# Second block's expert pairs in another order, and their loads written out

## The reference

```python
h2 = rms_norm_2(x, norm2_g)
# group: argmax of h2 @ w_group + b_group; in it the top 2 of h2 @ w_expert + b_expert
g, u = h2 @ w_gate[group, e], h2 @ w_up[group, e]      # 1024 -> 256
x = x + sum(gate[e] * ((silu(g) * u) @ w_down[group, e]))   # 256 -> 1024
```

## Time and profile before

| | |
|---|---|
| median of 3 runs | 1562.14 us |
| lowest and highest | 1559.04 and 1563.06 us |
| time of the profiled execution | 1566.48 us |
| its span in the trace | 1564.7 us |
| PE busy | 1338.8 us, 86% |
| DVE, ACT, POOL busy | 454.9, 379.1, 47.8 us |
| moved from memory | 476.71 MB, 306 GB/s over the span |

### The profile page before, as it was taken

The page is one execution under the profiler, slowest core; times in us unless marked ns, Lnnn a source line. Parts: engine busy times, 40 slices in busy tenths (PEclk is TensorE's granted clock), DMA queues, the critical chain, the costliest instruction groups (busy, mean ns, idle before and its releaser), DMA issues.

```text
span 1564.7 us, 31839 instructions
## 1 busy us (share of the span) xinstructions
PE 1338.8 (86%) x12460; PEld 697.1 (45%) x12461; DVE 454.9 (29%) x1358; ACT 379.1 (24%) x730; POOL 47.8 (3%) x74
## 2 busy tenths in 40 slices
PE   4999987988666786799999898987899899999986
PEld 3655444454232343355556544433337454443432
DVE  1102466442121121233344533111122544212112
ACT  2101235112111111122223322222132432222212
POOL 1100030000000000000000000000000000000000
PEclk8899999999898899899999899999899999999988
DMA  9968412769999999989784277999992435679996
GB/s 360 359 253 265 113 28 95 272 254 418 417 419 416 419 417 418 418 359 417 299 314 161 81 282 279 418 417 418 418 396 94 166 129 217 255 289 419 416 419 254
DMA packets 104049, 479.45 MB, mean 306 GB/s; under 512 B 9521, under 2 KB 20110, under 8 KB 70910
## 3 DMA queue, kind: packets, MB, share of 16 engines
q1 hardware_dynamic: 100256, 469.66, 76.0%
q0 software_dynamic: 2688, 7.43, 1.7%
q10 hardware_dynamic: 1054, 1.63, 0.3%
HBM read 476.71 MB, written 1.98 MB: 306 GB/s over the span
## 4 chain that ended last, share of the span: by engine, by line
PE 58%; SPq 18%; DMA 12%; DVE 6%; issue 4%; ACT 2%; ACTq 0%; DVEq 0%; PEldq 0%
SPq L518 18%; PE psum L1199 6%; PE psum L1938 6%; DMA store<-in_w_up 6%; PE psum L774 5%; PE psum L1190 5%; PE psum L1175 5%; PE psum L1148 4%; DMA store<-in_w_expert_up 4%; PE psum L1210 3%; PE psum L1934 3%; PE psum L1217 2%; PE psum L1470 2%; PE psum L1458 2%; PE psum L1503 1%
## 5 line engine op out<-in xcount | busy, mean ns | idle before, releaser
L1190 PE MATMUL psum<-store 128*32 128x256 f32 x2624 | 176.7, 411 | 58.9 <-DMA store<-in_w_expert_up 57.5
L1199 PE MATMUL psum<-store 128*32 128x256 f32 x2432 | 156.4, 414 | 25.0 <-DMA store<-in_w_up 23.1
L1348 DVE TENSOR_TENSOR store<-store,psum 128x128 f32<-128x128 f32 x79 | 22.7, 288 | 464.8 <-ACT store L1280 464.4
L1190 PEld LDWEIGHTS psum<-store 128*32 128x32 f32 x2624 | 79.8, 115 | 139.4 <-DMA store<-in_w_expert_up 85.7
L1175 PE MATMUL psum<-store 32*128 32x256 f32 (+1 forms) x992 | 129.5, 478 | 2.0 <-ACT store L1286 1.4
L1148 PE MATMUL psum<-xn,store 128*32 128x256 f32 (+1 forms) x992 | 130.0, 490 | 1.3 <-DVE store L1311 1.2
L1199 PEld LDWEIGHTS psum<-store 128*32 128x32 f32 x2432 | 88.7, 119 | 83.1 <-issue 34.5
L1280 ACT ACTIVATE store<-psum 128x128 f32<-128x128 f32 x79 | 21.9, 277 | 405.2 <-PE psum L1190 276.8
L1280 ACT ACT_TABLE_LOAD x79 | 101.4, 1283 | 52.7 <-issue 52.0
L1938 PE MATMUL psum<-store 128*128 128x512 f32 x224 | 97.7, 593 | 0.0
L1175 PEld LDWEIGHTS psum<-store 32*128 32x128 f32 (+1 forms) x992 | 59.2, 191 | 75.2 <-issue 69.6
(11 more groups left out here) (357 smaller groups left out, 1441.4 us busy)
## 6 DMA issues: line engine op xcount, KB each, us to landing
store<-in_w_expert_up SPq DMA_DIRECT2D x128, 1024.0 KB, 22.3
store<-in_w_expert_down SPq DMA_DIRECT2D x64, 1024.0 KB, 22.4
store<-in_w_gate SPq DMA_DIRECT2D x64, 1024.0 KB, 17.8
store<-in_w_up SPq DMA_DIRECT2D x64, 1024.0 KB, 19.6
store<-in_w_down SPq DMA_DIRECT2D x64, 1024.0 KB, 20.2
store<-in_w_mod SPq DMA_DIRECT2D x12, 2048.0 KB, 14.3
store<-in_w_in SPq DMA_DIRECT2D x6, 2048.0 KB, 12.2
store<-in_w_out SPq DMA_DIRECT2D x6, 2048.0 KB, 15.2
```

What stands on the lines that cost most here:

```text
L1190: mm = pe.matmul(out_(j), chosen_rows(k, 0), wt[:, kk, :, j, :], start=(k == 0), stop=(k == KD - 1))
L1199: mm = pe.matmul(out_(j), chosen_rows(k, e), wt, start=(k == 0), stop=(k == KD - 1))
```

## The change

In both layers of the second block the rounds take the pairs in the order 0, 4, 8, 12, 1, 5, 9, 13, 2, 6, 10, 14, 3, 7, 11, 15: one pair of each group in turn. The loads read their sources by that order; `ranks`, the gates and `extra` are written in that order too, by views that permute the columns. Two vector operations (L1024 and L1043) become two each, one for each tile of 128 tokens, for the second block alone. The ranks' first step writes into `chosen` in place. For the second block the loop over loads on SP is replaced by 72 loads in a row, with addresses known beforehand; the waits before them count the same.

```diff
-        def expert_loads(sp, plan, sources, turned, dense_done, adds):
+        def expert_loads(sp, plan, sources, turned, dense_done, adds, order=None):
             stage = plan.stage(sources[0].shape[0])
+            nth = order or list(range(stage.rounds))
...
-                load(i, j, sources[j][r])
+                load(i, j, sources[j][nth[r]])
...
-                load(2, j, sources[j][3])
-            turns = (stage.rounds - 1) // TURN - 1
-            with sp.Fori(0, turns) as turn:
+                load(2, j, sources[j][nth[3]])
+            turns = 0 if order else (stage.rounds - 1) // TURN - 1
+            if turns:
+                with sp.Fori(0, turns) as turn:
...
             for r in range(TURN * (turns + 1) + 1, stage.rounds):
                 for j, src in enumerate(sources):
                     sp.wait_ge(*stage.freed(r - TURN, j))
-                    load((r - 1) % TURN, j, src[r])
+                    load((r - 1) % TURN, j, src[nth[r]])
...
-            link(dve.scalar_tensor_tensor(ranks[:, 0:NT, 0:NE], r[:, 0:NT, :], 1.0, chosen, ALU.add, ALU.mult))
-            link(dve.tensor_scalar(ranks[:, 0:NT, 0:NE], ranks[:, 0:NT, 0:NE], -1.0, None, ALU.add))
+            link(dve.scalar_tensor_tensor(chosen, r[:, 0:NT, :], 1.0, chosen, ALU.add, ALU.mult))
+            if which == 1:
+                link(dve.tensor_scalar(ranks[:, 0:NT, 0:NE], chosen, -1.0, None, ALU.add))
+            else:
+                for t in range(NT):
+                    ins_ = dve.tensor_scalar(woven(ranks[:, t, 0:NE]), chosen[:, t, :].rearrange("p (g b e) -> p g b e", g=NG, b=NG),
+                                             -1.0, None, ALU.add)
+                link(ins_)
+
+        def woven(x):
+
+            return x.rearrange("p (b g e) -> p g b e", b=NG, g=NG)
...
+            else:
+                for t in range(NT):
+                    ins_ = dve.tensor_tensor(woven(ranks[:, NT + t, 0:NE]), rest4[:, t].rearrange("p g (b e) -> p g b e", e=2),
+                                             first5[:, t, 0, 0:NG].unsqueeze(2).unsqueeze(3).broadcast_to([P, NG, NG, 2]), ALU.mult)
+                link(ins_)
...
-                link(dve.tensor_reduce(extra_m[:, 0:NE // at_once], extra_f.rearrange("p (b e) -> p b e", e=at_once), AX,
-                                       ALU.max))
+                link(dve.tensor_reduce(extra_m.rearrange("p (b g) -> p g b", b=NG),
+                                       extra_f.rearrange("p (g b e) -> p g b e", g=NG, b=NG), AX, ALU.max))
...
-                expert_loads(sp, plan, second_sources(layer), (sems["q_sb"], NT * (1 + layer)), 2 + layer, NT * (3 + 2 * layer))
+                pairs = [NG * g + b for b in range(NG) for g in range(NG)]
+                expert_loads(sp, plan, second_sources(layer), (sems["q_sb"], NT * (1 + layer)), 2 + layer, NT * (3 + 2 * layer),
+                             pairs)
```

More of the change, by code:

```diff
@@ L543, in expert_loads @@
                 sp.wait_ge(*stage.freed(0, j))
-                load(2, j, sources[j][3])
-            turns = (stage.rounds - 1) // TURN - 1
-            with sp.Fori(0, turns) as turn:
[L547 to L552, removed]
+                load(2, j, sources[j][nth[3]])
+            turns = 0 if order else (stage.rounds - 1) // TURN - 1
+            if turns:
+                with sp.Fori(0, turns) as turn:
+                    for i in range(TURN):
+                        for j, src in enumerate(sources):
+                            sem, count = stage.freed(1 + i, j)
+                            sp.wait_ge(sem, turn * (TURN * stage.used(j)[1]) + count)
+                            load(i, j, src[bass.ds(turn * TURN + (TURN + 1 + i), 1)][0])
             for r in range(TURN * (turns + 1) + 1, stage.rounds):
@@ L1022, in route_dve, with route_gates_dve @@
             r = ps[5][:, 0:3 * NE].rearrange("p (n e) -> p n e", e=NE)
-            link(dve.scalar_tensor_tensor(ranks[:, 0:NT, 0:NE], r[:, 0:NT, :], 1.0, chosen, ALU.add, ALU.mult))
-            link(dve.tensor_scalar(ranks[:, 0:NT, 0:NE], ranks[:, 0:NT, 0:NE], -1.0, None, ALU.add))
+            link(dve.scalar_tensor_tensor(chosen, r[:, 0:NT, :], 1.0, chosen, ALU.add, ALU.mult))
[8 more added lines that the diff above has]
+            return x.rearrange("p (b g e) -> p g b e", b=NG, g=NG)
         def group_marks():
             return first5[:, :, 0, 0:NG].unsqueeze(3).broadcast_to([P, NT, NG, EG])
-        def route_gates_dve(dve, at, link):
+        def route_gates_dve(dve, at, link, which):
             wide = lambda x: x.unsqueeze(2).unsqueeze(3).broadcast_to([P, NT, NG, EG])
@@ L1042, in route_gates_dve @@
             link(dve.tensor_tensor(rest4, rest4, second4, ALU.add))
-            link(dve.tensor_tensor(ranks[:, NT:, 0:NE].rearrange("p t (g e) -> p t g e", g=NG), rest4, group_marks(),
-                                   ALU.mult))
+            if which == 1:
+                link(dve.tensor_tensor(ranks[:, NT:, 0:NE].rearrange("p t (g e) -> p t g e", g=NG), rest4, group_marks(),
+                                       ALU.mult))
+            else:
[3 more added lines that the diff above has]
+                link(ins_)
         def extra_rounds_dve(dve, at, link, which):
@@ L1370, in experts_dve @@
                 dve.wait_ge(sems["gate_moe_in"], 64)
-            route_gates_dve(dve, at, link)
+            route_gates_dve(dve, at, link, which)
             current(dve.tensor_copy(it[:, NT:, :], ranks[:, NT:, 0:at_once]))
```

## The result

The changed kernel takes 1538.78 us (median of 4 runs, 1538.19 to 1540.42); the one before took 1562.60 us beside it (1559.04 to 1563.62). The ratio is 0.9843, with a 95% interval of 0.9821 to 0.9864. Timed again in two later sessions it gave 0.9868 (0.9848 to 0.9888) and 0.9847 (0.9830 to 0.9864). A median of 1540.2 had been forecast, within a range of 1534 to 1549.

The account below looks back on a forecast made before the run. Transfers and the matmul engine were taken to bound the kernel in turn. Layer 1's 15.9 us plus layer 0's 6.6 less 0.6 for vector operations gave 21.9 us, so a median of 1540.2 us, range 1534 to 1549.

Parts of the forecast that it names:

- What bounds: Second block's rounds: PE and transfers bound in turn; six double rounds (pairs needing a second pass), two in layer 0, four in layer 1.
- Part one: Layer 1's rounds: spreading double rounds starts loads sooner, PE runs through, and the last pass starts 15.9 us earlier.
- The tightest place: Layer 1, behind double round 4: round 7's loads go out at 1385.4, 0.5 us before the stream needs them.
- Part two: Layer 0's rounds: double rounds at 11 and 15 let round 15 start 8.3 us earlier, less 1.7: 6.6 us.
- slow first pass: Layer 0's round 15: a pass that waited for data has slower up matmuls, taking back 1.7 us.
- cushion of 4.6 us: Layer 0: lag from double round 11 that can grow by 4.6 us before it touches round 15.
- Part three: Loads on SP, 72 a layer: removing their loop and register offset is priced at nothing, under 2 us if cover fails.
- Part four: Vector engine, ranks and gate product in two operations each: 0.15 us at two places in two layers, 0.6 us cost.
- The sum: Whole kernel: 15.9+6.6-0.6 = 21.9 us gain, profiled span to 1542.8, median to 1540.2.
- slower transfers: Rival, weight loads of both layers: new address order slows the stream, 1554 at 392 GB/s, 1600 at 350; chance 0.05.
- a layer 0 without gain: Rival, layer 0's rounds: only layer 1 pays, layer 0 gives 0 to 3 us, time 1544 to 1547; chance 0.07.
- signs of being wrong: Full-stretch rate below 416 to 419 GB/s, layer 1 waiting on w_up after round 7, or 155.1 us between layers changing over 1 us.

Follow-up runs that it names:

- layer1_doubles_4to7: Changed kernel, but layer 1 goes group by group in the order 1, 0, 2, 3, its double rounds at 4 to 7: 1545.66 us, ratio 0.9885.
- after_again: The changed kernel itself, unaltered, timed again in a later session against the kernel before: 1544.23 us against 1563.77, ratio 0.9868.
- two single-layer kernels: New order in one layer only, the other keeping pairs 0 to 15 with loads written out: layer 1 alone 1547.31 us, layer 0 alone 1558.63 us.
- before: The kernel without the change, the baseline: 1562.60 us beside the changed kernel's first timing.
- loads_written_out: Kernel before with only the second block's loads written out, in the old order: 1565.75 us against 1563.77, ratio 1.0003.

## Why the prediction was right, point by point

**What bounds.** Six double rounds were to move and did: layer 0's to 11 and 15, layer 1's to 0, 4, 8 and 12. The rows that answer to the earlier trace rows, layer 0's two and layer 1's last:

```profile
1068.55 0.16 DVE L1361 TENSOR_SCALAR store<-store 128x4 f32<-128x4 f32 x1
...
1129.78 0.16 DVE L1361 TENSOR_SCALAR store<-store 128x4 f32<-128x4 f32 x1
...
1468.11 0.17 DVE L1361 TENSOR_SCALAR store<-store 128x4 f32<-128x4 f32 x1
```

**Part one, layer 1: 15.9 forecast, 16.2 measured** (16.1 to 16.2 in the other four profiles with this order there). The windows of the layer, up to the closing of the stream and from there to the last pass:

```profile
1303.20:1327.00 23.80, 22.81 (x248) 10.53 (x252) 7.79 (x34) 6.20 (x11) 0.54 (x1) 1.00 0.27 92
1327.00:1514.50 187.50, 174.94 (x1718) 76.54 (x1707) 37.98 (x136) 50.26 (x84) 0.00 (x0) 1.00 1.00 411
```

They answer to these of the kernel before, which had the transfers at half use for 80 us and PE at 87% and a granted clock of 0.94 for the 148 us after them:

```profile
1315.10:1395.00 79.90, 77.13 (x793) 33.95 (x794) 18.86 (x76) 21.65 (x37) 0.53 (x1) 1.00 0.52 204
1395.00:1542.60 147.60, 128.00 (x1170) 55.76 (x1166) 26.02 (x95) 35.38 (x59) 0.00 (x0) 0.94 1.01 414
```

The tightest place, round 7's loads, was forecast at 70.3 us after the first pass (1385.4 in the old times); they were issued at 1373.45, which is 70.2 after 1303.21:

```profile
1373.45 0.34 SPq L519 DMA_DIRECT2D store<-in_w_gate  x1
```
```profile
1371.00:1374.00 3.00, 3.00 (x46) 1.41 (x39) 0.61 (x3) 0.29 (x2) 0.00 (x0) 1.00 1.02 410
1374.00:1377.00 3.00, 3.00 (x16) 0.96 (x11) 0.09 (x1) 0.60 (x1) 0.00 (x0) 1.00 1.06 429
```

No gap opened. A small one would have cost little: in `layer1_doubles_4to7` some 20 us of expected gaps cost the layer 2.9 us, with a stream that closed 5 us sooner.

**Part two, layer 0: 6.6 forecast, 5.9 measured.** The double round 11 was absorbed as worked out, and round 15 waited for its own data. The starts are those of rounds 11, 14 and 15:

```profile
1074.63 5.61 PE L1217 MATMUL psum<-store 128*32 128x256 f32 x64 [3.99 <-DMA store<-in_w_up]
...
1120.79 3.66 PE L1217 MATMUL psum<-store 128*32 128x256 f32 x64
1134.76 6.25 PE L1217 MATMUL psum<-store 128*32 128x256 f32 x64 [2.72 <-DMA store<-in_w_up]
```

Round 15's data came 60.1 us behind round 11's, four steps of 15.03 against 15.08, and round 15 itself started 8.5 us nearer to layer 0's first pass, where 8.3 had been worked out. The mis-sized term is the slow first pass: 1.7 us had been taken, and 1147.65-1134.76 = 12.9 us stands against 10.3 unwaited, so 2.6. All of it lies in the pass's up matmuls (6.25 us against 3.66), and the granted clock goes with it. Their window, and the same round in `after_again`:

```profile
1134.76:1141.01 6.25, 6.25 (x66) 2.83 (x68) 0.00 (x0) 0.00 (x0) 0.00 (x0) 0.58 1.03 397
```
```profile
1138.31 3.66 PE L1217 MATMUL psum<-store 128*32 128x256 f32 x64 [2.97 <-DMA store<-in_w_up]
```
```profile
1138.31:1141.97 3.66, 3.66 (x66) 2.05 (x68) 0.00 (x0) 0.00 (x0) 0.00 (x0) 1.00 1.03 406
```

The granted clock was 0.58 after a wait of 2.7 us in one and 1.00 after 3.0 us in the other, so the length of the wait alone does not decide it. In the eight profiles with layer 0 in this order the slow first pass cost 2.5 to 2.8 in six, 1.5 in one and 0 in one (`after_again`, whose layer 0 took 206.4). Round 14 had been expected to start at its data, and did not: round 11's first pass was slow too (5.61 us), and round 14 started some 1 us after its data; round 15's cushion of 4.6 us hid it.

**Part three, the loop: 0 forecast, 0 measured** (ratio 1.0003), with its one experiment above.

**Part four, the vector engine: 0.6 forecast, about 0.3 measured.** Timeline of DVE:

```profile
934.13 0.27 DVE L1030 TENSOR_SCALAR store<-store 128x32 f32<-128x32 f32 x2
...
941.25 0.29 DVE L1060 TENSOR_TENSOR store<-store 128x32 f32<-128x32 f32 x2
```

The two operations overlap, so a pair takes 0.27 and 0.29 us where one took 0.19 and 0.23: 0.14 a layer. These are durations. The prediction put both places on the path between router and first marks, but the gate product at 941.25 stands behind the first pass's start at 939.13, as it did before. The step to the second pass grew by 0.03 us in layer 0 and by 0.07 in layer 1, so even 0.3 may be more than the time saw.

**The sum.** 21.9 forecast and 21.65 measured from layer 0's first pass on, 21.6 by the two single-layer kernels, 19.5 to 24.5 by three medians. That the sum agrees to 0.3 us is partly luck: layer 1 gave 0.3 more than forecast and layer 0 0.7 less. For the profiled execution a span of 1542.8 had been forecast, and it was 1536.6; the 6.2 us between them are the 6.45 ahead of layer 0, which the prediction had left as they were. The chance of 0.05 for slower transfers and of 0.07 for a layer 0 without gain found nothing in their favour. None of the signs of being wrong showed: the full slices ran at 416 to 420 GB/s, no pass of layer 1 waited for a load, and the stretch between the layers changed by 0.43 us.

## What to carry to other kernels

Where a ring of buffers stands between a steady stream and rounds of uneven length, sort each round by its sign against the stream: long rounds early hold buffers and starve the stream, long rounds at the end have nothing to hide behind, and in between they are free while the consumer's lag is less than what the shorter rounds behind them give back. Work the order out round by round (start of the pass, freeing of its slots, landing of the next data); here the profiles of the kernel before and of the changed one gave the layer's time for eight placements within 2.5 us each. Mixing heavy and light does not choose what comes last: the two orders that put a single round last in layer 0 took 8.4 and 11.1 us less there than the one that put a double round last. How the orders fare on another routing no run here shows.

## What the runs showed of the hardware

The same stretch differs from execution to execution. In thirteen profiles, layer 0's first pass starts between 938.5 and 945.6 us. One place of it is seen in the two profiles of before and after, the first matmuls of the attention's projection (before: L1549; after: L1569), with the windows that hold exactly these matmuls:

```profile
862.39 5.46 PE L1549 MATMUL psum<-store 128*128 128x512 f32 x8 [2.20 <-DVE store L1700]
```
```profile
862.39:867.85 5.46, 5.46 (x9) 3.04 (x10) 0.00 (x0) 0.00 (x0) 0.00 (x0) 0.50 0.00 0
```
```profile
858.38 2.82 PE L1569 MATMUL psum<-store 128*128 128x512 f32 x8 [2.19 <-DVE store L1720]
```
```profile
858.38:861.20 2.82, 2.82 (x9) 1.76 (x10) 0.00 (x0) 0.00 (x0) 0.00 (x0) 1.00 0.00 0
```

After the same wait of 2.2 us the eight matmuls took 5.46 us in one and 2.82 in the other, at a granted clock of 0.50 and of 1.00: the same code meets 1.2 GHz in one execution and 2.4 in the other.

All thirteen profiles have this place, and it tells whether the change had a hand in the 6.45 us. They reach it between 857.8 and 864.4 us, ahead of layer 0's router and its rounds. The two kernels that write the ranks in one operation, `before` and `loads_written_out`, reach it at 862.39 and 862.83, inside what the others show. From there to layer 0's first pass ten profiles take 80.1 to 81.0 us, whichever kernel they are of; the other three take 82.2, 82.3 and 83.2, and in just these the eight matmuls were slow (4.22, 4.49 and 5.46 us). So of the 6.45 us some 4.0 came ahead of the place and 2.4 behind it, and the profiles show no share of the change beyond some tenths. The one operation that the change edits ahead of the place, the first block's ranks written in place, is in the eleven and not in the two.

With such places in it, a single profile of this kernel can't carry a difference under some 7 us by its span. By stretches it can carry less where the matmul engine does not wait: layer 1 took 211.3 to 211.4 us in all five profiles that had its new order with group 0 first and two vector operations. Layer 0, which waits for loads, took 206.4 to 208.7 us in the eight profiles of its new order.
